# GpSimd takes over the short convolution, the zero fills, four weight splits and one residual scaling

## The reference, cut to what matters

```python
y_a = conformer_conv(a_val, a_gate, ...)          # 31-tap depthwise convolution of a_val * sigmoid(a_gate)
y_b = diff_attention(q1, q2, k1, k2, v, ...)      # softmax attention, 4 heads, two maps each
y_c = spatial_gating(u, sv, ...)
y_d = bg * depthwise_conv(cg * xin, conv_d_w)     # the short convolution: 3 taps
x = x + mod_x[2] * (concatenate([y_a, y_b, y_c, y_d]) @ w_out)
```

## Time and profile before

| what | value |
|---|---|
| median of three runs | 1733.29 us |
| span of the profiled execution (first to last instruction) | 1729.7 us |
| PE, DVE, ACT, POOL busy | 95%, 51%, 32%, 4% of the span |
| chain that ended last | PE 70%, DMA 21%, DVE 6%, ACT 2% |
| granted PE clock | 0.991 of full speed |

### The profile page before, as it was taken

The page is one execution under the profiler, slowest core; times in us unless marked ns, Lnnn a source line. Parts: engine busy times, 40 slices in busy tenths (PEclk is TensorE's granted clock), DMA queues, the critical chain, the costliest instruction groups (busy, mean ns, idle before and its releaser), DMA issues.

```text
span 1729.7 us, 30518 instructions
## 1 busy us (share of the span) xinstructions
PE 1639.7 (95%) x13052; PEld 1253.7 (72%) x13052; DVE 879.3 (51%) x1719; ACT 546.9 (32%) x947; POOL 63.4 (4%) x120
## 2 busy tenths in 40 slices
PE   6999999999989999888989999989999999999998
PEld 4789777555555555555555557958999998699998
DVE  4415554325643121221122126997888787787776
ACT  3234323412411100000000004456555544474443
POOL 0001002000000000000000000000000000000000
PEclk9999999999999899999999999999999999999999
DMA  9955749999999999999999999564455352755430
GB/s 388 400 202 189 291 202 408 406 424 425 424 424 424 424 425 424 425 425 426 424 424 425 425 424 371 188 243 147 156 186 194 146 218 80 288 186 183 173 140 24
DMA packets 65989, 527.63 MB, mean 305 GB/s; under 512 B 6585, under 2 KB 16057, under 8 KB 28752
## 3 DMA queue, kind: packets, MB, share of 16 engines
q1 hardware_dynamic: 51312, 471.18, 67.4%
q0 software_dynamic: 14560, 54.75, 7.9%
HBM read 523.81 MB, written 1.05 MB: 303 GB/s over the span
## 4 chain that ended last, share of the span: by engine, by line
PE 70%; DMA 21%; DVE 6%; ACT 2%; issue 1%; SPq 0%; DVEq 0%; ACTq 0%
PE bank L916 69%; DMA big<-in_w_exp_down 9%; DMA big<-in_w_exp_up 5%; DMA big<-in_w_exp_gate 3%; DMA big<-in_w_ada 1%; DVE big L2941 1%; DVE w_lo L2333 1%; DMA big<-in_ada_half 1%; DMA big<-in_ada_w 1%; DVE big L2333 1%; DVE big L2998 1%; ACT w_hi L2152 0%; DVE big L3073 0%; DVE big L3057 0%; DVE big L2812 0%
## 5 line engine op out<-in xcount | busy, mean ns | idle before, releaser
L916 PE MATMUL bank<-big 128*32 128x352 f32 (+11 forms) x7456 | 957.9, 413 | 75.6 <-DMA big<-in_w_exp_down 25.1
L916 PEld LDWEIGHTS bank<-big 128*32 128x32 f32 (+5 forms) x7456 | 578.3, 142 | 437.6 <-issue 280.6
L2333 DVE TENSOR_TENSOR w_lo<-big,w_hi 128x1024 fp32r<-128x1024 f32 x212 | 257.6, 1221 | 120.5 <-ACT w_hi L2293 53.1
L916 PE MATMUL bank<-h_lo,w_hi 128*128 128x256 f32 (+1 forms) x1040 | 296.1, 285 | 0.0
L916 PE MATMUL bank<-h_hi,w_hi 128*128 128x256 f32 (+1 forms) x896 | 257.2, 287 | 6.3 <-DVE h_lo L2333 2.8
L916 PE MATMUL bank<-h_hi,w_lo 128*128 128x256 f32 (+1 forms) x896 | 255.0, 285 | 0.0
L916 PEld LDWEIGHTS bank<-h_lo,w_hi 128*128 128x128 f32 x1040 | 198.5, 191 | 0.7
L2333 DVE TENSOR_TENSOR big<-big 128x256 f32<-128x256 f32 (+7 forms) x223 | 115.2, 525 | 155.2 <-ACT big L2128 132.4
L916 PEld LDWEIGHTS bank<-h_hi,w_hi 128*128 128x128 f32 x896 | 171.5, 191 | 10.1 <-DVE h_lo L2333 4.8
L2293 ACT ACTIVATE w_hi<-big 128x1024 fp32r<-128x1024 f32 x120 | 127.0, 1058 | 146.9 <-PE bank L916 146.9
L916 PEld LDWEIGHTS bank<-h_hi,w_lo 128*128 128x128 f32 x896 | 171.8, 192 | 0.7
(11 more groups left out here) (267 smaller groups left out, 1356.7 us busy)
## 6 DMA issues: line engine op xcount, KB each, us to landing
big<-in_w_exp_gate SPq DMA_DIRECT2D x64, 1408.0 KB, 21.4
big<-in_w_exp_up SPq DMA_DIRECT2D x64, 1408.0 KB, 20.9
big<-in_w_exp_down SPq DMA_DIRECT2D x48, 1536.0 KB, 21.0
big<-in_mlp_w SPq DMA_DIRECT2D x32, 2048.0 KB, 8.2
big<-in_w_in SPq DMA_DIRECT2D x17, 2048.0 KB, 10.5
big<-in_u_w POOLq DMA_DIRECT2D x64, 512.0 KB, 9.3
big<-in_w_ada SPq DMA_DIRECT2D x12, 2048.0 KB, 14.0
big<-in_ada_w SPq DMA_DIRECT2D x12, 2048.0 KB, 9.5
```

The lines of the kernel that those rows point to most:

```text
L916: return nc.tensor.matmul(o, l, r, start=start, stop=stop)
L2333: return V.tensor_tensor(o, a, b, op)
```

## The change

GpSimd's list gets a loop over the two layers behind its last DMA issue. In it GpSimd fills `glu` and `cx` with zeros; in layer 0 multiplies the residual by its weight (eight `tensor_scalar` of 128 x 256) and by the reciprocal root (four `tensor_tensor` of 128 x 512); makes the short convolution as three `tensor_scalar` and two `tensor_tensor` of 128 x 256 for each of the two halves, each waiting for the one before; and makes the low parts of units 20 to 23 (four `tensor_tensor` of 128 x 1024). DVE's instructions for all that go. A new semaphore `side_out` counts GpSimd's steps; DVE waits on it before the products into `glu` and `cx` and before `accd * bgf`, PE (and SP, which reloads the slot) together with the low parts of units 20 to 23. ACT waits for the scaled residual before it overwrites `rs`. Two older semaphores are merged into one (`state_out`), which frees the number for `side_out`; that moves no instruction.

```diff
+        SIDE_UNITS = (20, 24)
+        def side_units(j):
+            return min(max(j - SIDE_UNITS[0], 0), SIDE_UNITS[1] - SIDE_UNITS[0])
         def dve_split(layer, j):
-            return split_no(layer, j) + LEAD
+            return split_no(layer, j) + LEAD - side_units(UNITS) * layer - side_units(j)
         def units_split(layer, j):
-            return [(S("w_lo_ready"), dve_split(layer, j))]
+            side = [(S("side_out"), side_w(layer, j))] if side_units(j) else []
+            return [(S("w_lo_ready"), dve_split(layer, j))] + side
...
 # GpSimd, behind its last DMA issue
+            def side(ins):
+                sides[0] += 1
+                ins.then_inc(S("side_out"), 1)
+            def side_taps(m, w):
+                for x in range(3):
+                    o = tap_t if x else accd[:, m, :]
+                    side(G.tensor_scalar(o, cx[:, m, 0, x:x + T], w[:, m, x:x + 1], None, ALU.mult))
+                    if x:
+                        pool.wait_ge(S("side_out"), sides[0])
+                        side(G.tensor_tensor(accd[:, m, :], accd[:, m, :], tap_t, ALU.add))
+                        pool.wait_ge(S("side_out"), sides[0])
+            for layer in range(2):
+                if layer:
+                    pool.wait_ge(S("y_out"), 64 + 4)
+                else:
+                    pool.wait_ge(S("c_used"), 92)
+                side(G.memset(glu, 0.0))
+                side(G.memset(cx, 0.0))
+                if layer == 0:
+                    pool.wait_ge(S("h_scaled"), 2 * KT)
+                    for t in range(KT):
+                        i_ = G.tensor_scalar(resid[:, t, 0:T], resid[:, t, 0:T], v0("norms", 8, KT)[:, 2, t:t + 1], None, ALU.mult)
+                    side(i_)
+                    pool.wait_ge(S("side_out"), sides[0])
+                    pool.wait_ge(S("r1_ready"), 1)
+                    for t in range(0, KT, 2):
+                        G.tensor_tensor(resid[:, t:t + 2, 0:T], resid[:, t:t + 2, 0:T], bc(rs[:, T:N2], 1, [P, 2, T]), ALU.mult) \
+                            .then_inc(S("x_in2"), 1)
+                pool.wait_ge(S("tile_out_D"), D_TILES_AFTER_OUT[layer] - KT)
+                for m in range(2):
+                    side_taps(m, v2(layer, "cdw", 2, 3))
+                for j in range(*SIDE_UNITS):
+                    pool.wait_ge(S("w_hi_ready"), split_no(layer, j + 1))
+                    side(G.tensor_tensor(w_split(w_lo, j), proj_unit(layer, j), w_split(w_hi, j).bitcast(F32), ALU.subtract))
...
 # DVE
-                V.memset(glu, 0.0)
-                link(V.memset(cx, 0.0))
...
                             dve.wait_ge(S("tile_out_A"), a_out)
+                            dve.wait_ge(S("side_out"), side_pads(layer))
...
-                        w_low(layer, 16 + NWB)
                 i_.then_inc(S("qk2_ready"), 1)
-                w_low(layer, 17 + NWB)
...
-                    if u < 4 and layer == 0:
-                        dve.wait_ge(S("r1_ready"), 1)
-                        for t in (2 * u, 2 * u + 1):
-                            V.scalar_tensor_tensor(resid[:, t, 0:T], resid[:, t, 0:T], v0("norms", 8, KT)[:, 2, t:t + 1],
-                                                   rs[:, T:N2], ALU.mult, ALU.mult).then_inc(S("x_in2"), 1)
-                        taps(cx, accd, v2(layer, "cdw", 2, 3), 0, 1, None)      # u == 0
-                        taps(cx, accd, v2(layer, "cdw", 2, 3), 1, 3, None)      # u == 1
-                        w_low(layer, 18 + NWB)                                  # u == 3
-                        dve.wait_ge(S("taps"), TAPS_AT[0])                      # u == 4
+                        dve.wait_ge(S("side_out"), side_d(layer))
-                        w_low(layer, 19 + NWB)                                  # u == 5
```

More of the change, by code:

```diff
@@ L340, in weights_to @@
             return mix[:, 4 - 2 * (u % 4 - 1):6 - 2 * (u % 4 - 1), 0:T]
+        tap_t = view(PERS + names2["wr"][0], T)
         part2, dg = view(PERS + V2_BASE + 2 * V2_N, 256), view(PERS + V2_BASE + 2 * V2_N + 256, 2, P)
@@ L501, in split_no, with side_pads, side_d, side_w @@
             return UNITS1 + UNITS * layer + j
+        SIDE_UNITS = (20, 24)
+        def side_units(j):
+            return min(max(j - SIDE_UNITS[0], 0), SIDE_UNITS[1] - SIDE_UNITS[0])
         def dve_split(layer, j):
-            return split_no(layer, j) + LEAD
+            return split_no(layer, j) + LEAD - side_units(UNITS) * layer - side_units(j)
+        def side_pads(layer):
+            return 2 if layer == 0 else side_w(0, UNITS) + 2
+        def side_d(layer):
+            return side_pads(layer) + 10 + (layer == 0)
+        def side_w(layer, j):
+            return side_d(layer) + side_units(j)
         def units_split(layer, j):
-            return [(S("w_lo_ready"), dve_split(layer, j))]
+            side = [(S("side_out"), side_w(layer, j))] if side_units(j) else []
+            return [(S("w_lo_ready"), dve_split(layer, j))] + side
         CONTEXT_AT = [(1 + x // 3, (1, 4, 9)[x % 3]) for x in range(KT)]
@@ L904, in _ @@
                 pool.dma_start(view(B3["ring"][0] + v % RING * 1024, 1024), src).then_inc(S(f"ring_full{v % RING}"), 16)
+            G = nc.gpsimd
+            sides = [0]
+            def side(ins):
[29 more added lines that the diff above has]
+                    side_taps(m, v2(layer, "cdw", 2, 3))
+                assert sides[0] == side_d(layer)
+                for j in range(*SIDE_UNITS):
+                    pool.wait_ge(S("w_hi_ready"), split_no(layer, j + 1))
+                    side(G.tensor_tensor(w_split(w_lo, j), proj_unit(layer, j), w_split(w_hi, j).bitcast(F32), ALU.subtract))
+                assert sides[0] == side_w(layer, SIDE_UNITS[1])
         @block.tensor
@@ L1234, in _ @@
             pe.wait_ge(S("rope_out"), 4)
-            pe.wait_ge(S("Sr_out"), 1)
+            pe.wait_ge(S("state_out"), 3)
             def ret_scores(hh):
@@ L1984, in _ @@
                 act.wait_ge(S("mixer_ps"), hp2 + 4)
-                A(og[:, hp2:GH:2, :], PB[4 + hp2][:, :].rearrange("p (a b) -> p a b", a=2), ACT.Copy).then_inc(S("j_out"), 1)
+                A(og[:, hp2:GH:2, :], PB[4 + hp2][:, :].rearrange("p (a b) -> p a b", a=2), ACT.Copy).then_inc(S("state_out"), 1)
             for hh in range(RH):
@@ L1995, in _ @@
                 i_ = A(Sr[:, d, :, :], PB[4 + d][:, :].rearrange("p (a b) -> p a b", a=4), ACT.Copy)
-            i_.then_inc(S("Sr_out"), 1)
+            i_.then_inc(S("state_out"), 1)
             act.wait_ge(S("hn_step"), 2)
@@ L2248, in _ @@
                 act.wait_ge(S("oss_ps"), layer + 2)
+                if layer == 0:
+                    act.wait_ge(S("x_in2"), KT // 2)
                 A(rs, PB[4], ACT.Sqrt, bias=eps_t, scale=1.0 / 64).then_inc(S("o_rms"), 1)
@@ L2560, in _ @@
             dve.wait_ge(S("mixer_ps"), 3)
-            dve.wait_ge(S("j_out"), 2)
+            dve.wait_ge(S("state_out"), 2)
             for hp in range(2):
@@ L3001, in mixer_step @@
                 def mixer_step(u):
-                    if u < 4 and layer == 0:
-                        dve.wait_ge(S("r1_ready"), 1)
-                        for t in (2 * u, 2 * u + 1):
-                            V.scalar_tensor_tensor(resid[:, t, 0:T], resid[:, t, 0:T], v0("norms", 8, KT)[:, 2, t:t + 1],
-                                                   rs[:, T:N2], ALU.mult, ALU.mult).then_inc(S("x_in2"), 1)
                     if u == 0:
-                        dve.wait_ge(S("tile_out_D"), d_out[0])
-                        taps(cx, accd, v2(layer, "cdw", 2, 3), 0, 1, None)
                         dve.wait_ge(S("sv_std"), layer + 2)
@@ L3103, in _ @@
                 if layer == 0:
-                    dve.wait_ge(S("x_in2"), KT)
+                    dve.wait_ge(S("x_in2"), KT // 2)
                 if layer:
```

## The result

The changed kernel takes 1747.7 us (median of 6 runs, 1744.8 to 1749.5) against 1733.6 us before: ratio 1.0078 (95% interval 1.0067 to 1.0088), so 11.6 to 15.3 us slower. The forecast was 1744.0, slower. The profiled span goes from 1729.7 to 1744.8 us.

What follows compares the result with a forecast made beforehand. PE bounds the kernel; a relieved DVE can pay only in layer 0, at most 3.5 us. Layer 0's 13.1 - 2.9 = +10.2 and layer 1's +0.5 give span 1740.4, plus 3.6 for the median: 1744.0 us, range 1729.5 to 1756.

Steps and rivals of the forecast that it cites:

- Zero fills: Memsets moved to GpSimd's expert loop; DVE loses two ahead of an idle wait: no gain or loss.
- Residual scaling: Layer 0, from the norm: its last two 512-column GpSimd instructions hold DVE, +2.3 us (ends 0 and 7.8).
- Taps: Layer 0's short convolution: ten GpSimd instructions hold DVE 0.58 us each, +5.8 us (ends 3.6 and 10.1).
- The price rule: DVE loses a GpSimd instruction's duration less 0.14 us when both read SBUF.
- Low parts: Layer 0, DVE's last taps and rotation: three GpSimd low parts hold DVE, +6.2 us (ends 3.2 and 8.2).
- unit 20: DVE's own low part of unit 20 leaves layer 0's rotation: -1.2 us.
- Rotation: Layer 0: the rotation's end (`qk2_ready`) comes 13.1 us later, and PE stands idle for it.
- Attention units: Layer 0: DVE loses 8.2 us of work, but only PE's waits of 2.9 us can return: -2.9 us.
- Layer 1: Rotation some 3 us late, but mostly hidden by DMA waits of 6.37 and 10.84 us: +0.5 us (ends 0 and 3.3).
- rival 1: DVE is not held and GpSimd is late instead: -3.5 us, 1729.8 us; chance 0.24.
- Rival 2: DVE is held only by the long low parts: +2.6 us, 1735.9 us, no change that can be told; chance 0.07.
- Rival 3: GpSimd `tensor_scalar` with a per-partition scalar takes four times the two-operand form, 2.9 us: about +51, 1784 us; chance 0.05.

Runs made afterwards that it cites:

- c1_pe_busy: Changed kernel plus 24 (layer 1: 8) small matmuls, results unused, where PE waits for the rotation: 1741.3 us, ratio 1.0043.
- p1_read_two: Kernel before plus 16 unneeded GpSimd additions of two 128x256 SBUF operands in layer 0's convolution: 1740.9 us.
- p3_write_only: Kernel before plus 32 unneeded GpSimd memsets of 128x256, which read nothing, in layer 0's convolution: 1733.5 us, ratio 0.9997.
- b1_scale_early: Kernel before with zeros on GpSimd, DVE's residual scaling in its idle time ahead of the convolution, unit 20's low part behind the rotation: 1732.2 us, ratio 0.9985.
- e4_zeros_only: Changed kernel with all but the zero fills back on DVE: 1734.1 us, ratio 0.9998.
- p2_read_one: Kernel before plus 16 unneeded GpSimd products of one 128x256 SBUF operand with a per-partition scalar in layer 0's convolution: 1736.6 us.

## Why the prediction was right, and where it was not

The direction and the mechanism hold: GpSimd's reads hold DVE's SBUF instructions on the one stretch where DVE sets PE's pace. By its steps:

- **Zero fills, 0.** Right (ratio 0.9998 with them alone).
- **Residual scaling, +2.3.** Right: the low part beside it takes 1.59 us instead of 1.22 and the two first taps 1.38 each instead of 0.41, 2.3 us together. It ends at 1093.7, 1091.1 on the clock of before, where 1091 stood. That end is luck in part: GpSimd's twelve instructions are 12.5 us of work at their undisturbed lengths (0.92 and 1.29) instead of 10.8, and lost 4.6 us to DVE instead of 6.4. Undone, it gave 3.3 in A.
- **Taps, +5.8.** Mis-sized: 2.7. The price rule (duration less 0.14) came from one instance. Beside an unbroken row of taps an addition of 0.64 us costs 0.38, so the part that DVE does not lose is 0.26 here; that DVE makes its start in it is a reading, not shown. A product with a scalar costs 0.14 to 0.22, though it takes 0.97 us instead of the 0.72 taken.
- **Low parts, +6.2, and unit 20, -1.2.** Right: 2.15 + 2.13 + 1.30 = 5.6 and -1.1. An undisturbed one takes 2.35 (2.2 taken).
- **Rotation, +13.1.** 9.4 (A); the four terms, 2.3 + 2.7 + 5.6 - 1.1, add up to 9.5. Of the signs named, the durations grew; but PE's wait ahead of the scores is 5.8 us, not 10 or more, since it meets 3.5 us of the delay earlier, in two waits for low parts within the convolution, which the forecast had left out.
- **Attention units, -2.9.** The step that failed. The waits went as said (2.9 to 0.6), but PE's own work took 2.2 us longer at half clock behind its wait of 5.8 us. The forecast had created that wait and priced only its length. With PE kept busy (c1_pe_busy) B fell by 2.3 us.
- **Layer 1, +0.5.** 1.9 (D 1.7, E 0.2). The rotation's holds, 1.5 and 2.1 us, brought the first scores 1.7 us later. The first DMA wait is hidden behind that and the chain runs over one, not over two as I had said; but the second ends 0.9 us later, and PE's work behind it took 7.16 instead of 6.21 us at a clock of 0.76 instead of 1.00. That fall is not shown to be the change's: over some 21 us of the same stretch p1_read_two, p3_write_only and b1_scale_early have a clock of 0.92, and e4_zeros_only and p2_read_one 1.00.
- **Not in the forecast:** +1.5 in C and +2.5 ahead of the norm. Neither is shown to be the change's. PE waits 1.37 to 1.41 us in C in the thirteen profiles without added matmuls there, and the clock behind it is 0.86 in four of them, among them p3_write_only and b1_scale_early. The norm's first product stands between 1069.4 and 1072.5 in all profiles.

9.4 - 0.1 + 1.5 + 1.9 + 2.5 = 15.2, with rounding the 15.1 us of the span. The terms that the forecast had come to 11.2 of these against its 10.7: too much for the taps, and too little for the clock and layer 1, nearly cancelled, so the total was better than its terms. That is luck, and the other 4.0 us have no cause shown.

Two side sums of the prediction are off, and nothing else hangs on them: with the lower ends for `tensor_scalar` (0 and 3.6) the total is +6.2, not +6.4; and in rival 1 a loss of 0.1 us per instruction still gives 15 x 0.1 - 3.6 = -2.1, the terms reach 0 at 0.24.

Rival 1 (DVE not held) falls by p1_read_two. Rival 2 (only the long ones hold) falls too: the short ones cost 2.7 us. Rival 3 had a core of truth: on GpSimd a `tensor_scalar` is slower than the two-operand form, 0.93 against 0.70 us in the two added rows, but not four times.

The Trainium skill (GPSIMD Engine Reference, section 4.1 Engine selection) has one-input operations on GpSimd at roughly line rate. The trace does not agree for this form: 0.93 us against DVE's 0.35.

The Trainium skill (SBUF — State Buffer, section Who interferes with whom) says that a DVE instruction with two SBUF inputs contends with a GpSimd instruction that reads SBUF and not with one that only writes. The added reads (0.39 us each) and writes (0) agree. The Trainium skill (SBUF — State Buffer, section SBUF: two separate sides) has the ports that the two engines share held for the whole instruction. A product of 0.93 us that costs 0.2 does not agree, and in the changed kernel's trace a tap with two SBUF operands begins and ends (1105.62 to 1106.31 us) while such a product runs (1105.51 to 1106.49).

## What to carry to other kernels

Before work goes to an idle engine, look at what the busy one reads beside it: GpSimd's reads were paid on DVE's taps, low parts and rotation, and a chain of short steps with idle time between them gave no cover. A wait that the change gives to TensorE can cost its length and then a half clock behind it, as the 5.8 us here did. DVE's own gaps on the same path were the better place for the work: the version that used them, and moved one low part, gained 0.15% at best, where the change cost 0.78%.

## What the runs showed of the hardware

- The hold goes both ways: beside DVE's work GpSimd's products with a scalar took up to 2139 ns (973 at the least), its additions 1375 (635).

```profile
L937 POOL TENSOR_SCALAR big<-big x12: 973/1004/2139, 1100.8 to 1442.5; 128x256 f32<-128x256 f32 x12
```

```profile
L940 POOL TENSOR_TENSOR big<-big x8: 635/637/1375, 1104.0 to 1443.6; 128x256 f32<-128x256 f32 x8
```

- Two SBUF operands are not needed on DVE's side: `tensor_scalar` with one was held as well (407 to 1383 ns, and 0.29 to 2.35 us), while `tensor_tensor` with one of its operands in PSUM was not (684). Nor is every form with one SBUF operand held: `reciprocal` took 1746 ns beside GpSimd's products (1076.51 to 1086.56 us) and 1745 in the kernel before.

```profile
L3005 DVE TENSOR_SCALAR big<-big x4: 407/894/1383, 1091.1 to 1424.5; 128x256 f32<-128x256 f32 x4
```

```profile
1078.53 1.75 DVE L2987 RECIPROCAL big<-big 128x256 f32<-128x256 f32 x1
```

- With the same wait of 1.4 us (1.37 to 1.41) in front of the same products TensorE's clock fell in some profiles and not in others: 0.86 over the 12 us behind it in four of thirteen, 1.00 in nine.
